# Opening of a float32 decoder block on one core: loads reordered, tokens turned and multiplied in two halves, the bias table's product first

## The reference, cut to what matters

```python
def rms_norm(x, g):
    xf = x.astype(jnp.float32)
    y = xf * lax.rsqrt(jnp.mean(xf * xf, axis=-1, keepdims=True) + EPS)
    return (y * g.astype(jnp.float32)).astype(x.dtype)
...
    h = rms_norm(x, pre_mix_g[l])
    proj = h @ w_in[l]
    q, k, v, u_pool, u_conv, g_logits = jnp.split(proj, IN_SPLITS, axis=-1)
    attn = moba_attention(heads(q), heads(k), heads(v), rel_bias)   # adds table_t[h, t5_bucket(distance)]
    pool = pool_mixer(u_pool, w_pool_g[l], pool_scale[l]) @ w_pool_o[l]
    conv = conv_module(u_conv, w_dw[l], b_dw[l], conv_ln_g[l], conv_ln_b[l]) @ w_conv_o[l]
    merged = gates[:, :, 0] * attn + gates[:, :, 1] * pool + gates[:, :, 2] * conv
    x = x + rms_norm(merged @ w_out[l], post_mix_g[l])
    h = rms_norm(x, pre_ffn_g[l])
    gt, up = jnp.split(h @ w_ffn_in[l], 2, axis=-1)
    f = (jax.nn.silu(gt) * up) @ w_ffn_out[l]
    x = x + rms_norm(f, post_ffn_g[l])
```

## Time and profile before

| | us |
|---|---|
| median of 3 runs | 713.23 (713.22 to 713.30) |
| the profiled execution, its own time | 715.35 |
| its span on the core | 713.5 |
| time around the span | 1.85 |

### The profile page before, as it was taken

How to read it: one execution, slowest core, us unless ns; L and a number is a source line. 1 busy time by engine, 2 the same in 40 slices (tenths; PEclk the granted TensorE clock), 3 DMA queues, 4 the chain that set the end, 5 groups by cost and what they waited for, 6 DMA issues and landing times.

```text
span 713.5 us, 11157 instructions
## 1 busy us (share of the span) xinstructions
PE 695.3 (97%) x3944; PEld 610.9 (86%) x3944; DVE 530.0 (74%) x763; ACT 352.2 (49%) x568; POOL 204.6 (29%) x178
## 2 busy tenths in 40 slices
PE   4999999999999999999999999999999999999996
PEld 3788888888888888888889889999999999888884
DVE  5437878657667566688475848888998897888997
ACT  6324544553544656224344435554555455656672
POOL 2024122222220000572124135645565450000125
PEclk9999999999999999999999999999999999999998
DMA  6337999999875222324511322233223325665563
GB/s 248 120 118 188 246 263 227 261 237 216 234 181 156 90 88 101 107 90 150 203 66 41 131 89 71 106 118 118 87 89 118 118 95 165 184 203 185 171 209 129
DMA packets 37752, 107.31 MB, mean 150 GB/s; under 512 B 4083, under 2 KB 4083, under 8 KB 37532
## 3 DMA queue, kind: packets, MB, share of 16 engines
q1 hardware_dynamic: 29708, 83.86, 34.8%
q0 software_dynamic: 8000, 23.07, 14.9%
q10 hardware_dynamic: 16, 0.02, 0.0%
HBM read 104.82 MB, written 25.19 MB: 182 GB/s over the span
## 4 chain that ended last, share of the span: by engine, by line
PE 88%; DVE 4%; issue 3%; DMA 2%; POOL 1%; ACT 1%; SPq 0%; DVEq 0%; POOLq 0%; ACTq 0%
PE bank L1542 28%; PE bank L1544 27%; PE bank L1543 27%; PE bank L1593 1%; DMA x_tok<-in_x_dram 1%; PE bank L1583 1%; PE bank L1584 1%; PE bank L1610 1%; DVE w_lo L990 1%; PE bank L1609 1%; DMA raw_pair<-in_w_ffn_in_dram 1%; DVE w_lo L1437 1%; POOL w_sum L549 0%; DVE s_lo L1447 0%; ACT junk L606 0%
## 5 line engine op out<-in xcount | busy, mean ns | idle before, releaser
L1542 PE MATMUL bank<-h_hi,w_hi 128*128 128x512 f32 (+1 forms) x424 | 162.7, 384 | 1.8 <-DVE h_lo L1018 1.8
L1543 PE MATMUL bank<-h_lo,w_hi 128*128 128x512 f32 (+1 forms) x424 | 160.7, 379 | 0.0
L1544 PE MATMUL bank<-h_hi,w_lo 128*128 128x512 f32 (+1 forms) x424 | 160.7, 379 | 0.0
L990 DVE TENSOR_TENSOR w_lo<-raw,w_hi 128x1024 fp32r<-128x1024 f32 x58 | 77.1, 1329 | 62.9 <-ACT w_hi L596 51.6
L1542 PEld LDWEIGHTS bank<-h_hi,w_hi 128*128 128x128 f32 x424 | 80.1, 189 | 16.2 <-issue 2.2
L1544 PEld LDWEIGHTS bank<-h_hi,w_lo 128*128 128x128 f32 x424 | 80.2, 189 | 15.2
L1543 PEld LDWEIGHTS bank<-h_lo,w_hi 128*128 128x128 f32 x424 | 80.3, 189 | 14.0
L1367 DVE TENSOR_TENSOR blk_lo<-raw_pair,blk_hi 128x512 fp32r<-128x512 f32 (+1 forms) x36 | 56.7, 1576 | 13.9 <-ACT blk_hi L844 13.9
L1542 PE MATMUL bank<-tm_hi,blk_hi 128*128 128x256 f32 x216 | 61.1, 283 | 0.0
L1543 PE MATMUL bank<-tm_lo,blk_hi 128*128 128x256 f32 x216 | 61.1, 283 | 0.0
L1544 PE MATMUL bank<-tm_hi,blk_lo 128*128 128x256 f32 x216 | 61.1, 283 | 0.0
(11 more groups left out here) (230 smaller groups left out, 1648.3 us busy)
## 6 DMA issues: line engine op xcount, KB each, us to landing
raw<-in_w_in_dram SPq DMA_DIRECT2D x42, 512.0 KB, 5.0
raw_pair<-in_w_ffn_in_dram SPq DMA_DIRECT2D x36, 512.0 KB, 3.8
comb<-in_w_ffn_out_dram POOLq DMA_DIRECT2D x30, 512.0 KB, 7.4
raw<-comb SPq DMA_DIRECT2D x20, 512.0 KB, 3.6
raw<-in_w_ffn_out_dram SPq DMA_DIRECT2D x15, 512.0 KB, 4.1
comb<-comb POOLq DMA_DIRECT2D x10, 512.0 KB, 5.5
raw<-in_w_branch_dram SPq DMA_DIRECT2D x8, 512.0 KB, 3.3
raw<-in_w_out_dram SPq DMA_DIRECT2D x8, 512.0 KB, 3.3
```

What stands on the lines that cost most here:

```text
L990: dve.tensor_tensor(dst, src_hi[0], src_hi[1], ALU.subtract).then_inc(lo_done, 1)
L1542: pe.matmul(dst, a_hi, b_hi, start=start, stop=False, skip_group_check=resumed)
L1543: pe.matmul(dst, a_hi, b_lo, start=False, stop=False, skip_group_check=resumed)
L1544: return pe.matmul(dst, a_lo, b_hi, start=False, stop=stop, skip_group_check=resumed)
```

## The change

Eight edits belong together.

- SP loads token tiles 0 and 1, then unit 0, then `vec`, then tiles 2 and 3, then the other units; `const` has a semaphore of its own and comes after unit 2. ACT issues the one-hot matrix and the bias table as its first instructions.
- DVE scales the bias table and, before it touches x, waits for the table's product and copies it out of banks 6 and 7; PE makes that product before the first transpose. SP issues the store of `bias_vec`, once both copies are done.
- Token tiles 0 and 1 are scaled by DVE as before, tiles 2 and 3 by POOL.
- Tokens are handled in two halves of 256. A turned block k of a half lies in half a bank: banks 0 to 3 for the first half, 7, 0, 1, 2 for the second.
- ACT writes `h_hi` for the first half after the squares of all four tiles, then splits unit 1, then the second half. DVE follows with `h_lo`, waiting for `h_hi` in twos.
- PE's unit 0 works on the first half, with tile 2 turned after k = 5 and tile 3 after k = 7, and then on the second half. It writes bank 4; the first six units use banks 4, 5, 6.
- ACT splits `w_hi` of unit 0 between the squares of tiles 1 and 2.
- `w_lo` of unit 1 is made by POOL; DVE waits for it and passes the count on with a one-column memset.

```diff
-            for t in range(TOK):
+            def load_x(t):
                 sp.dma_start(x_tok[:, t, :], x[0, t * P:(t + 1) * P, :]).then_inc(x_full[t], 16)
...
+            load_x(0)
+            load_x(1)
+            load(0, 0, w_in[first[0] // P], whole)
+            sp.dma_start(vec[:, :], vecs).then_inc(vec_full, 16)
+            load_x(2)
+            load_x(3)
             for u, col in enumerate(first):
-                load(u, u % RING, w_in[col // P], whole)
-                if u == 0:
-                    sp.dma_start(vec[:, :], vecs).then_inc(vec_full, 16)
-                    sp.dma_start(const[:, :], pool_const).then_inc(vec_full, 16)
+                if u:
+                    load(u, u % RING, w_in[col // P], whole)
                 if u == 2:
-                    sp.dma_start(onehot_sb[0:33, :], onehot).then_inc(tab_full, 16)
-                    sp.dma_start(table[0:32, :], rel_bias).then_inc(tab_full, 16)
+                    sp.dma_start(const[:, :], pool_const).then_inc(const_full, 16)
+                    sp.wait_ge(vec_read, 2)
+                    sp.dma_start(bias_scratch, bias_vec[0:8, :]).then_inc(bias_stored, 16)
                     sp.wait_ge(prep_done, 1)
...
                 rsqrt(t, 4 + t, 8 + t, 1.0 / D_MODEL, EPS).then_inc(rstd_done, 1)
+                if t >= 2:
+                    pool.wait_ge(rstd_done, t + 1)
+                    pool.tensor_scalar(x_tok[:, t, :], x_tok[:, t, :], stat[:, 8 + t:9 + t], None, ALU.mult)\
+                        .then_inc(x_scaled, 1)
+            pool.wait_ge(hi_done, 2)
+            pool.tensor_tensor(w_lo[:, 1, :], raw[:, 1, :], w_hi[:, 1, :].bitcast(F32), ALU.subtract).then_inc(w1_lo_done, 1)
...
+            act.dma_start(onehot_sb[0:33, :], onehot).then_inc(tab_full, 16)
+            act.dma_start(table[0:32, :], rel_bias).then_inc(tab_full, 16)
             for t in range(TOK):
                 act.wait_ge(x_full[t], 16)
                 square_sum(x_tok[:, t, :], t, junk_x[:, :])
-            hi(0, 0)
-
-            act.wait_ge(vec_full, 32)
-            act.wait_ge(xt_done, TOK)
-            for k in range(KT):
-                act.activation(h_hi[:, k, :], bank[k][:, :], ACT.Copy, scale=vec[:, V_PRE + k:V_PRE + k + 1])\
-                   .then_inc(h_hi_done, 1)
-            hi(1, 1)
+                if t == 1:
+                    hi(0, 0)
+
+            act.wait_ge(vec_full, 16)
+            for half, cols in enumerate(TOKEN_HALVES):
+                for k in range(KT):
+                    act.wait_ge(xt_done, XT_TURNED[half] + k // 2)
+                    act.activation(h_hi[:, k, cols], turned(half, k), ACT.Copy, scale=vec[:, V_PRE + k:V_PRE + k + 1])\
+                       .then_inc(h_hi_done, 1)
+                if half == 0:
+                    hi(1, 1)
...
-            for t in range(TOK):
+            dve.wait_ge(tab_full, 32)
+
+            dve.tensor_scalar(table[0:32, :], table[0:32, :], 8.0, None, ALU.mult).then_inc(prep_done, 1)
+            dve.wait_ge(vec_mm, 1)
+            dve.tensor_copy(bias_vec[0:8, 0:SEQ], bank[6][0:8, :]).then_inc(vec_read, 1)
+            dve.tensor_copy(bias_vec[0:8, SEQ:BIAS_LEN], bank[7][0:8, 0:P]).then_inc(vec_read, 1)
+            for t in range(2):
                 dve.wait_ge(rstd_done, t + 1)
                 dve.tensor_scalar(x_tok[:, t, :], x_tok[:, t, :], stat[:, 8 + t:9 + t], None, ALU.mult).then_inc(xn_done, 1)
             lo_int(0)
-            dve.wait_ge(vec_full, 32)
-            for k in range(KT):
-                dve.wait_ge(h_hi_done, k + 1)
...
+            dve.wait_ge(vec_full, 16)
+            for half, cols in enumerate(TOKEN_HALVES):
+                for k in range(KT):
+                    dve.wait_ge(h_hi_done, KT * half + (k | 1) + 1)
+                    dve.scalar_tensor_tensor(out=h_lo[:, k, cols], in0=turned(half, k),
+                                             scalar=vec[:, V_PRE + k:V_PRE + k + 1], in1=h_hi[:, k, cols].bitcast(F32),
+                                             op0=ALU.mult, op1=ALU.subtract).then_inc(h_lo_done, 1)
+            dve.wait_ge(w1_lo_done, 1)
+            dve.memset(spare[:, 0:1], 0.0).then_inc(lo_done, 1)
...
+            pe.wait_ge(prep_done, 4)
+            pe.matmul(bank[6][0:8, :], table[0:33, :], onehot_sb[0:33, 0:SEQ], start=True, stop=True)
+            pe.matmul(bank[7][0:8, 0:P], table[0:33, :], onehot_sb[0:33, SEQ:BIAS_LEN], start=True, stop=True)\
+              .then_inc(vec_mm, 1)
+
+            def turn_x(t):
+                if t < 2:
+                    pe.wait_ge(xn_done, t + 1)
+                else:
+                    pe.wait_ge(x_scaled, t - 1)
+                for k in range(KT):
+                    if t == 2 and k == 0:
+                        pe.wait_ge(vec_read, 2)
+                    if t == 2 and k % 2 == 0 and k:
+                        pe.wait_ge(h_lo_done, k)
+                    ins = pe.transpose(turned(t // 2, k)[:, t % 2 * P:(t % 2 + 1) * P], x_tok[:, t, k * P:(k + 1) * P],
+                                       ident[:, :])
...
+            turn_x(0)
+            turn_x(1)
+            pe.wait_ge(lo_done, 1)
+            for half, cols in enumerate(TOKEN_HALVES):
                 for k in range(KT):
-                    ins = pe.transpose(bank[k][:, t * P:(t + 1) * P], x_tok[:, t, k * P:(k + 1) * P], ident[:, :])
-                ins.then_inc(xt_done, 1)
-            for u in range(FIRST_UNITS):
+                    pe.wait_ge(h_lo_done, KT * half + k + 1)
+                    ins = mm3(bank[FIRST_BANK][:, cols], w_hi[:, 0, k * P:(k + 1) * P], w_lo[:, 0, k * P:(k + 1) * P],
+                              h_hi[:, k, cols], h_lo[:, k, cols], k == 0, k == KT - 1)
+                    if half == 0 and k == 5:
+                        turn_x(2)
+                if half == 0:
+                    turn_x(3)
+            ins.then_inc(unit_done, 1)
+            for u in range(1, FIRST_UNITS):
...
+FIRST_BANK = 4
+TURN_BANKS = [(0, 1, 2, 3), (7, 0, 1, 2)]
+TOKEN_HALVES = (slice(0, TOK_HALF), slice(TOK_HALF, SEQ))
+XT_TURNED = (2, 7)
```

More of the change, by code:

```diff
@@ L297, in whole, with turned @@
             return tile
+        def turned(half, k):
+            return bank[TURN_BANKS[half][k // 2]][:, k % 2 * TOK_HALF:(k % 2 + 1) * TOK_HALF]
         def k2(tile):
@@ L1565, in _ @@
                     pe.wait_ge(*FIRST_FREED[u - RING])
-                unit(u % RING, bank[u % RING], h_hi, h_lo,
-                     before_k=(lambda k: pe.wait_ge(h_lo_done, k + 1)) if u == 0 else None).then_inc(unit_done, 1)
-                if u == 0:
-                    pe.wait_ge(prep_done, 4)
-                    pe.matmul(bank[6][0:8, :], table[0:33, :], onehot_sb[0:33, 0:SEQ], start=True, stop=True)
-                    pe.matmul(bank[7][0:8, 0:P], table[0:33, :], onehot_sb[0:33, SEQ:BIAS_LEN], start=True, stop=True)\
-                      .then_inc(vec_mm, 1)
+                unit(u % RING, bank[FIRST_BANK + u % RING], h_hi, h_lo).then_inc(unit_done, 1)
             def scores(p, i):
@@ L1733, in turn_x1 @@
             def turn_x1(t):
-                pe.wait_ge(xn_done, TOK + t + 1)
+                pe.wait_ge(xn_done, TOK // 2 + t + 1)
                 for k in range(KT):
@@ L1842, in _ @@
                             ins = down(n, i, ph, k, t)
-                        if n == turned and t == 0:
+                        if n == turn_unit and t == 0:
                             ins.then_inc(u4_full, 1)
```

32 lines of the change are left out of this document (12 added, 20 removed).

## The result

The changed kernel took 716.81 us (median of 5 runs, 715.97 to 718.2) against 713.3 us (5 runs, 713.22 to 713.49) for the kernel before on the same chip: a ratio of 1.005, interval 1.0039 to 1.0061. It is slower by 0.5%, outside the range, and on the side that had a chance of 0.12.

What follows compares the result with a forecast made beforehand. PE was taken as full from its first matmul, so only unit 1's start counted: -1.17, -1.6, -1.4, +1.6, +1.3, +0.4 give -0.9 us (22.9 against 23.81), span 712.6, median 712.3 us; own range 711.7 to 713.0, all runs 711.4 to 714.6.

Steps and rivals of the forecast that it cites:

- the side that had a chance of 0.12: Whole kernel: a time above 714.66 us, slower by more than 0.2%; chance 0.12.
- The reference: Start of unit 1 in the profiled kernel before, 23.81 us, taken as the time to beat; median 2.12 us below profiled time.
- no slow stretch in unit 0: Unit 0 on PE: the half-rate stretch of 8 matmuls in the old trace would vanish, -1.6 us.
- POOL's price and its independence of DVE: POOL's scaling of tiles 2 and 3: taken as 1.3 us each, between 0.75 and 2.4.
- Both are covered: Tile 3's scaling and `w_lo` of unit 1 on POOL would be ready before PE needs them, the first by only 0.2 us.
- even at 2.4: POOL's scaling at its upper price of 2.4 us: tile 2 scaled from 11.7 to 14.1, tile 3 from 15.1 to 17.5.
- The wait for the table: Opening: table lands at 4.5, DVE free at about 8.1, transposes of tiles 0 and 1 until 12.3, first matmul at 13.9.
- Rival 2: Opening: the table lands at 7.9 and holds up x, first matmul 1.9 us later, 714.2 us; chance 0.12.
- The turning of tile 3 and the gap: Between unit 0's halves: tile 3 turned from 17.7, PE going on at 19.8 after a gap of 1.3 us.
- Outside the span: Time outside the span, taken as unchanged: span 712.6 us, profiled execution's own time 714.4.
- rival 1: Unit 0: the clock falls as before, its first-half matmuls run at 0.21 us each, 713.4 to 714.0 us; chance 0.28.
- rival 4: Start of unit 1: it waits for POOL's `w_lo`, POOL's large instructions taking 3.4 us each, 713.2 us; chance 0.05.

Runs made afterwards that it cites:

- no_pool: The changed kernel with no large instruction on POOL: DVE scales all four tiles and makes `w_lo` of unit 1 between the halves; 715.76 us, ratio 1.0029.
- table_first_only: The kernel before with the table part alone: ACT loads it first, PE's product precedes the transposes, DVE copies it before scaling x; 715.62 us, ratio 1.0026.
- table_loads_only: The kernel before with only the loads of one-hot matrix and table moved to ACT's first instructions; 713.64 us, ratio 1.0005.
- after_again: The changed kernel run once more without any edit; 717.03 us, ratio 1.0054.
- before_again: The kernel before run once more without any edit, as a control; 713.61 us, ratio 1.0006.
- order_look: Second trace of the kernel before with only SP's new load order and unit 0's hi part made between the squares; ratio 1.0052.
- halves_only: The changed kernel with the table part undone: SP loads it after unit 2, product after unit 0; 717.22 us, ratio 1.0056.
- dve_scales: The changed kernel with the scalings of tiles 2 and 3 back on DVE, POOL keeping `w_lo` of unit 1; 717.31 us, ratio 1.005.

## Why the prediction was wrong

**The reference (failed, 2.1 us).** The sum credited 1.6 us for "no slow stretch in unit 0" and then took off another 2.12 us because the profiled execution lay that far above the median. Both were one thing. The execution's own time less its span was 1.85, and the 80 others have 1.74 to 1.88: profiling added nothing, this execution was merely a slow one (unit 1 at 23.74 instead of 22.36, the rest behind it 0.3 us longer), and the median had never paid for it. The span of 713.5 plus 1.85 against a median of 713.23 could have told so before any run: the usual span had to be near 711.4. With 22.4 as what unit 1 had to beat, the same sum of 22.9 reads +0.5 us, about 713.8.

**POOL's price and its independence of DVE (failed, 1.4 us).** The opening's schedule missed by 1.87 us: unit 1 at 24.77, not 22.9. `no_pool` splits that. Without large work on POOL unit 1 starts at 23.34, 0.44 behind the forecast; so the step that failed is "Both are covered". It put the scaling at 1.3 us, within bounds of 0.75 and 2.4; it took 2.85, above the upper one. And it let POOL run beside DVE without a term for it: POOL's 128x1 instruction at 10.39 took 1.76 us instead of 0.19 and ended at 12.15, with DVE's work on x and `w_lo` (12.10), so that the first scaling began at 12.90 instead of 11.7. Against the case "even at 2.4", with tile 3 scaled at 17.5, that is 1.2 for the start and twice 0.45 for the price: 19.6, and PE turned tile 3 at 19.69 instead of 17.7.

**The wait for the table (failed, 0.6 us at the first matmul).** The table landed at 6.2, not 4.5: 4.8 us behind its issue, between the two bounds, and the lower one had been taken. The copies cost 0.8 together, as taken. DVE was free at 9.57, not 8.1, and the transposes ended at 14.1, not 12.3. The first matmul came at 14.50 instead of 13.9: 0.6 us of the 1.5 came through, since ACT starts `h_hi` (12.92) on the first blocks while PE turns the rest. Rival 2 put its turning point at a landing of 6.1, and 6.2 is there, but its account has the first matmul 0.1 us behind the last transpose and would give 14.2; the trace has 0.4. `table_first_only` and `table_loads_only` show that it is the wait and not the loads.

**The rest of the schedule,** against the trace of after:
- *Loads.* Tile 3 was squared from 10.41, not after 11.0, the forecast's lower bound being 10.7; tiles 0 and 1 came late (squared from 4.93 and 6.40, not 3.9 and 5.2). Neither shows in the time, since DVE waits for the table.
- *Up to the end of the first half*, +0.25: k = 6 and 7 took 0.8 to 0.96 instead of 0.7. k = 5 came 2.33 us after the start, as forecast 2.3, and tile 2 took 0.79, as forecast 0.8.
- *The turning of tile 3 and the gap* took 1.88 us from 19.69 to 21.57, against 2.1; *the second half* 3.20 against 3.1.

In PE's list these add up to 0.6 + 0.25 + 1.1 (the wait for POOL) - 0.1 = 1.85 of the 1.87. The first three are not separate costs: POOL's end sets 19.69 whatever PE loses before it, as `after_again` shows.

**Outside the span (not foreseen, 0.7 us).** 1.8 assumed, a median of 2.5 found. The forecast of 712.3 and the 716.81 measured are 4.5 us apart: 1.6 in the span (the 1.87 less 0.3 by which the rest behind unit 1 was shorter than in the profiled execution of before), 2.1 in the reference, 0.7 outside, and 0.1 of rounding. For the 0.7 no step of the prediction had a term, and its cause is open.

**Right.** DVE's and ACT's pace for 256 columns (3.23 and 3.02 us for 8, 0.39 and 0.37 each); unit 0 at 0.12 us a matmul in the trace of after, so that rival 1 did not come there (it came in part in `after_again`, hidden by the wait for POOL); `w_lo` of unit 1 hidden in time; the loads on ACT's queue free for tile 3; unit 1 not held up, so that rival 4 did not come; no change behind unit 1. And the second 16 transposes of `before_again` took 2.62 us after 3.64 for the first, with nothing but transposes ahead of them. The Trainium skill, "TensorE: Matmul & The Clock Gate", Part 4, says that transposes do not count as PE being busy in the same way; the trace differs from it, with those two numbers, and so does unit 0 of after and of `before_again`, which ran at full rate from its first matmul (0.12 and 0.23 us apart) with little but transposes ahead. `after_again`, where it began at 0.21, fits the rule; what sets the rate from one execution to the next is open.

**How the parts go together.** Alone, against the usual span of 711.6, the table part costs 2.2 us, the load order 3.2, unit 0's halves on PE 2.8 and POOL's subtraction 1.2; all of the change costs 2.7. They are not a sum, since they wait for the same thing: in `no_pool` the four squares end at 11.4, and ACT waits until 12.82 for transposes that DVE's wait for the table holds up, so later tiles cost nothing there. The change with the old load order was not run. Of the 13 variants none came clearly below before; one, `table_loads_only`, is level with it. In the four versions of the changed kernel without the early product the first matmul came at 12.44 to 13.60 instead of 15.52, and in three of their traces the matmuls behind it ran at half rate, which gave back 1.3 us or more. The kernel before overlaps the landing of x, its squares, scalings and transposes closely: moving work into that stretch pushed the first matmul back, made another engine wait, or met the slow rate.

## What to carry to other kernels

Check a profiled execution against the median before building on it: own time less span shows what lies outside, and if the rest doesn't fit the median, what is odd in that trace (here a slow stretch of 1.6 us) is no saving to be had. Before giving an idle POOL work that runs beside DVE, list what DVE does at that time from SBUF to SBUF: a hidden microsecond moved there came back as one on the path. And a wait put ahead of a pipeline that hides loads, squares and transposes in each other can cost more than its own length, since the overlap goes with it. Last, before adding up delays along one engine's list, ask which of them the next wait would have swallowed.

## What the runs showed of the hardware

- POOL's multiplication of 128x1024 by a value per partition took 2.85 us in six instances in three traces, more than its subtraction of two tensors of that size (2.36 to 2.38) and 3.8 times DVE's 0.75.
- DVE and POOL instructions from SBUF to SBUF waited for each other's end, down to tiny ones: 32x8 elements in 2.24 us on DVE instead of 0.15, 128x1 in 1.76 on POOL instead of 0.19. A waiting instruction can be passed over: POOL's, started at 10.39 in after, was not let in between DVE's second scaling (until 10.97) and its subtraction, and ended only behind that (12.10). DVE's `h_lo`, which reads a PSUM bank, kept 0.39 us beside POOL's scaling at 12.90 to 15.75.
- The granted clock does not show every slow phase. In `order_look` it reads 1.00 for a stretch whose matmuls start 0.43 us apart (first row), in the earlier trace rows 0.50 for the same pace. The same holds for 256 columns: 0.21 us apart with 1.00 in `halves_only` (13 to 17 us), with 0.50 in `dve_scales` (23 to 25 us). The row of `order_look`, and the one behind it:

```profile
17.00:19.00 2.00, 1.96 (x5) 1.61 (x6) 2.00 (x4) 2.00 (x5) 0.00 (x0) 1.00 0.02 6
19.00:21.00 2.00, 2.00 (x9) 1.59 (x8) 2.00 (x4) 2.00 (x4) 0.00 (x0) 1.00 0.00 0
```

- Splitting 24 matmuls of one unit into 48 of half the width went with 0.5 to 1.1 us more outside the span, in 38 of 60 executions. Its cause is open.
